# Down projection of 128 expert chunks with the tokens on the partitions: stationary z, weights moving 512 wide, and a final norm by token

## The reference

```python
def peer_ffn(x, w_q, sub_keys, u_tab, v_tab):      # x is already normed
    ...
        gate = jax.nn.softmax(best_s, axis=-1)     # 8 heads x 16 experts a token
        ug = u_tab[eidx]
        vg = v_tab[eidx]
        hpre = jnp.einsum("nd,nhkd->nhk", xc, ug).astype(f32)
        act = (gate * jax.nn.gelu(hpre, approximate=False)).astype(x.dtype)
        return jnp.einsum("nhk,nhkd->nd", act, vg)

def second_block(x, ...):
    ...
        x = x + peer_ffn(h, ...)
    return rms_norm(x, norm_final)                 # x / sqrt(mean(x*x) + 1e-6) * norm_final
```

## Time and profile before

| | |
|---|---|
| median of 3 runs | 2049.94 us (2047.15 to 2049.99) |
| the profiled execution's own time | 2039.93 us |
| its span | 2037.9 us |
| mean granted TensorE clock | 0.943 of full speed |
| busy, share of the span | PE 93%, PEld 90%, DVE 70%, ACT 43%, POOL 1% |
| down chunks 0 to 63 (third stage) | from 1627.15 us |
| down chunks 64 to 127 (last stage) | 1831.98 to 2023.76 us |
| behind the last down matmul | 14.1 us |

### The profile page before, as it was taken

One profiled execution on the slowest core, in us unless ns is written; L12 is line 12 of the kernel. 1 busy time (PEld: TensorE's weight loads), 2 busy tenths in 40 slices (PEclk: granted clock), 3 DMA queues, 4 the chain that ended last, 5 costly groups with the idle time before them and its releaser, 6 DMA issues.

```text
span 2037.9 us, 41749 instructions
## 1 busy us (share of the span) xinstructions
PE 1889.6 (93%) x15336; PEld 1833.0 (90%) x15336; DVE 1424.0 (70%) x2437; ACT 874.7 (43%) x1317; POOL 19.3 (1%) x38
## 2 busy tenths in 40 slices
PE   7979997999799969997789979999999999999997
PEld 7969996988799959986679979999999999999997
DVE  5668886844688863447766549996888889994554
ACT  4333443443343335365444444455444344444443
POOL 0000000010000000000100000000000000000000
PEclk9989997976899989987999989999999999999999
DMA  5525553420455524430026624455444445554553
GB/s 199 185 98 183 181 181 100 156 93 12 164 185 185 182 87 144 135 114 1 1 83 202 200 95 145 165 165 185 166 165 166 164 150 168 167 165 167 176 176 109
DMA packets 80276, 293.70 MB, mean 144 GB/s; under 512 B 8960, under 2 KB 9120, under 8 KB 79824
## 3 DMA queue, kind: packets, MB, share of 16 engines
q1 hardware_dynamic: 79632, 289.96, 43.2%
q0 software_dynamic: 576, 2.79, 0.4%
HBM read 291.67 MB, written 1.05 MB: 144 GB/s over the span
## 4 chain that ended last, share of the span: by engine, by line
PE 81%; DVE 14%; ACT 3%; issue 2%; DMA 0%; DVEq 0%; ACTq 0%
PE ps L421 23%; PE ps L422 22%; PE ps L423 22%; DVE m L395 3%; PE ps L427 3%; PE ps L462 2%; PE ps L1492 1%; DVE m L1394 1%; DVE m L514 1%; PE ps L752 1%; DVE m L1390 1%; ACT m L383 1%; PE ps L751 1%; DVE m L1398 1%; DVE m L508 1%
## 5 line engine op out<-in xcount | busy, mean ns | idle before, releaser
L421 PE MATMUL ps<-m,m 128*128 128x256 f32 x4336 | 1252.7, 289 | 69.2 <-DVE m L522 33.8
L422 PE MATMUL ps<-m,m 128*128 128x256 f32 x4336 | 1235.0, 285 | 0.0
L423 PE MATMUL ps<-m,m 128*128 128x256 f32 x4336 | 1234.4, 285 | 0.0
L395 DVE TENSOR_TENSOR m<-m,m 128x1024 fp32r<-128x1024 f32 x546 | 663.1, 1222 | 432.1 <-ACT m L383 430.5
L421 PEld LDWEIGHTS ps<-m,m 128*128 128x128 f32 x4336 | 840.5, 194 | 83.6 <-issue 53.1
L422 PEld LDWEIGHTS ps<-m,m 128*128 128x128 f32 x4336 | 840.8, 194 | 0.6 <-issue 0.2
L423 PEld LDWEIGHTS ps<-m,m 128*128 128x128 f32 x4336 | 840.0, 194 | 0.0
L383 ACT ACTIVATE m<-m 128x1024 fp32r<-128x1024 f32 x546 | 576.1, 1056 | 472.5 <-PE ps L423 471.1
L1531 ACT ACTIVATE m<-ps 128x256 f32 (+1 forms) x128 | 49.2, 384 | 198.6 <-PE ps L423 198.5
L427 PEld LDWEIGHTS ps<-m,m 128*128 128x128 f32 (+1 forms) x412 | 64.3, 232 | 31.2 <-issue 11.4
L427 PE MATMUL ps<-m,m 128*128 128x128 f32 (+1 forms) x412 | 74.8, 338 | 14.1 <-ACT m L877 10.8
(11 more groups left out here) (198 smaller groups left out, 1131.2 us busy)
## 6 DMA issues: line engine op xcount, KB each, us to landing
m<-stream SPq DMA_DIRECT2D x546, 512.0 KB, 3.3
m<-alibi_t POOLq DMA_DIRECT2D x1, 1536.0 KB, 9.6
m<-con SPq DMA_DIRECT2D x1, 1353.0 KB, 10.1
m<-xT SPq DMA_DIRECT2D x1, 1024.0 KB, 4.9
y<-m SPq DMA_DIRECT2D x4, 256.0 KB, 2.4
m<-wcmpk POOLq DMA_DIRECT2D x1, 512.0 KB, 4.1
m<-wcmpv POOLq DMA_DIRECT2D x1, 512.0 KB, 4.8
m<-par SPq DMA_DIRECT2D x1, 178.0 KB, 5.4
```

Of the source, the lines that this page charges most:

```text
L395: nc.vector.tensor_tensor(w_lo[:, r, :], raw[:, r, :], w_hi[:, r, :].bitcast(F32), ALU.subtract)\
L421: nc.tensor.matmul(out, lhs[0], rhs[0], start=start, stop=False, **kw)
L422: nc.tensor.matmul(out, lhs[0], rhs[1], start=False, stop=False, **kw)
L423: return nc.tensor.matmul(out, lhs[1], rhs[0], start=False, stop=stop, **kw)
```

## The change

1. **Down turned round.** `down_tokens` replaces `down` for the 128 expert chunks. A 128-token half of z is stationary and the weights stream, 512 features wide: for each half c of the tokens, z hi with w hi, z hi with w lo, z lo with w hi, each over two halves of the features. That is 12 matmuls a chunk in place of 24, over the same number of columns. The four banks then hold tokens on the partitions.
2. **x by token.** `x_tokens_pe` puts x into these banks first, with 16 plain fp32 matmuls against the identity, behind the wait for the first z and ahead of the first chunk. `residual_dve` at the end goes.
3. **z ahead of the weights.** On ACT, z of chunk n is copied first and the hi part of weight chunk n + 1 is split behind it; before, the split stood ahead. DVE's splits in the last stage are one chunk earlier to match (`DOWN0 - 2` for `DOWN0 - 1`).
4. **Take in short runs.** The view of `emap` has the 8 tokens inside (runs of 8 floats), and PSUM is read in steps of 64 floats instead.
5. **Sum and norm by token.** ACT squares each half of the tokens and sums along the free dimension in the same instruction, the half c = 0 as soon as the last chunk has finished it; DVE's scale and inverse and ACT's root are then one column each, and four DVE instructions read PSUM and write y. The final norm's weights come as a row for every partition (`fin_row`, 512 KB), loaded by POOL's queue once the down chunks begin.

```diff
+    def x_tokens_pe(pe):
+        for c in range(2):
+            for k in range(KD):
+                nc.tensor.matmul(acc[:, 2 * c + k // 4, k % 4 * P:k % 4 * P + P], x[:, k, c * P:c * P + P], ident,
+                                 start=k % 4 == 0, stop=False, skip_group_check=True)
+
+    def down_tokens(pe, slot, src, final):
+        for c in range(2):
+            z = [v[:, c * P:c * P + P] for v in src]
+            for lhs, rhs, last in ((z[0], w_hi, False), (z[0], w_lo, False), (z[1], w_hi, final)):
+                for h in range(2):
+                    ins = nc.tensor.matmul(acc[:, 2 * c + h, :], lhs, rhs[:, slot, h * 512:h * 512 + 512],
+                                           start=False, stop=last, skip_group_check=True)
+            if final:
+                ins.then_inc(tok_done, 1)
+        if not final:
+            ins.then_inc(chunk_done, 1)
+
+    def final_act(act):
+        for c in range(2):
+            act.wait_ge(tok_done, c + 1)
+            nc.scalar.activation(y_out[:, c, :], acc_tok[:, c, :], ACT.Square, accum_out=y_sum[:, c:c + 1])\
+                .then_inc(tok_sum, 1)
+        for c in range(2):
+            act.wait_ge(tok_mean, c + 1)
+            nc.scalar.activation(y_r[:, c:c + 1], y_mean[:, c:c + 1], ACT.Sqrt).then_inc(tok_rms, 1)
+
+    def final_dve(dve):
+        for c in range(2):
+            dve.wait_ge(tok_sum, c + 1)
+            nc.vector.tensor_scalar(y_sum[:, c:c + 1], y_sum[:, c:c + 1], 1.0 / D, EPS, ALU.mult, ALU.add)\
+                .then_inc(tok_scaled, 1)
+            dve.wait_ge(tok_scaled, c + 1)
+            nc.vector.reciprocal(y_mean[:, c:c + 1], y_sum[:, c:c + 1]).then_inc(tok_mean, 1)
+        dve.wait_ge(s_fin, 16)
+        for c in range(2):
+            dve.wait_ge(tok_rms, c + 1)
+            for h in range(2):
+                f = slice(h * 512, h * 512 + 512)
+                nc.vector.scalar_tensor_tensor(y_out[:, c, f], acc_tok[:, c, f], y_r[:, c:c + 1], fin_row[:, f],
+                                               ALU.mult, ALU.mult).then_inc(y_normed, 1)
...
-        v = emap[:, half * HALF:half * HALF + HALF, bass.ds(st.lin(GT), GT)]
-        return v.rearrange("p a t -> p t a")
+        return emap[:, half * HALF:half * HALF + HALF, bass.ds(st.lin(GT), GT)]
...
-        nc.vector.scalar_tensor_tensor(v, ps[:, 6 + st.mod(2), :].rearrange("p (t a) -> p t a", t=GT), 1.0 / GSCALE, v, ALU.mult, ALU.mult)\
+        nc.vector.scalar_tensor_tensor(v, ps[:, 6 + st.mod(2), :].rearrange("p (t a) -> p a t", t=GT), 1.0 / GSCALE, v, ALU.mult, ALU.mult)\
...
-        down(pe, arrived(pe, st, a, b + DOWN0), ez[st.mod(2, a, b)], n == 0, n == NKEY - 1)
+        if n == 0:
+            x_tokens_pe(pe)
+        down_tokens(pe, arrived(pe, st, a, b + DOWN0), ez[st.mod(2, a, b)], n == NKEY - 1)
...
         def z(st, gates=None):
             if st.s >= 2:
-                walk_act(act, st, 1, DOWN0 - 2)
+                act.wait_ge(chunk_done, st.lin(1, DOWN0 - 1))
             if gates is not None:
                 act.wait_ge(gm_taken, gates)
             nc.scalar.activation(ez[st.mod(2)][0], emap[:, st.lin(1), :], ACT.Copy).then_inc(ez_hi, 1)
+            if st.s >= 2:
+                split_hi(act, st, 1, DOWN0 - 2 + RING)
...
             if not last:
                 z_rest(st, 2, 2)
-            walk_dve(dve, st, 2, DOWN0)
+                walk_dve(dve, st, 2, DOWN0)
...
         def fourth(st):
             z_rest(st, 1, 0)
-            walk_dve(dve, st, 1, DOWN0 - 1)
+            walk_dve(dve, st, 1, DOWN0 - 2)
...
+            pool.wait_ge(chunk_done, DOWN0)
+            pool.dma_start(fin_row, fin2).then_inc(s_fin, 16)
```

More of the change, by code:

```diff
@@ L135, with build @@
 GSCALE = 2.0 ** 14
-def build(nc, stream, xT, par, con, alibi_t, wg, wcmpk, wcmpv, peT, subk, y):
+def build(nc, stream, xT, par, con, alibi_t, wg, wcmpk, wcmpv, peT, subk, fin2, y):
     def sem(name):
@@ L185, in build @@
     x = l_.take(KD, T)
+    O_HH = l_.at
     h_hi, h_lo = l_.take(KD, T, dt=F32R), l_.take(KD, T, dt=F32R)
@@ L205, in build @@
     acc = ps[:, 0:4, :]
+    acc_tok = acc.rearrange("p (c h) f -> p c (h f)", c=2)
     f_ = Area(END - 8 * T)
@@ L286, in build @@
     ez = [(z_hi, z_lo), (at(O_NORM, T, dt=F32R), at(O_NORM + T, T, dt=F32R))]
+    y_out = at(O_HH, 2, D)
+    fin_row = at(O_HH + 2 * D, D)
+    y_sum, y_mean, y_r = (at(O_HH + 3 * D + 8 * i, 2) for i in range(3))
     s_x = sem("x_loaded")
@@ L345, in build @@
     s_y = sem("y_stored")
+    tok_done, tok_sum, tok_scaled = sem("token_half_summed"), sem("token_square_sum"), sem("token_mean_square")
+    tok_mean, tok_rms, y_normed = sem("token_mean_recip"), sem("token_rms_recip"), sem("y_part_normed")
+    s_fin = sem("final_weight_loaded")
     NCH = CH["end"]
@@ L517, in norm_dve @@
         if hb is None:
-            dve.wait_ge(x_normed, KD if n < 7 else 2 * KD)
+            dve.wait_ge(x_normed, KD)
             return
@@ L1556, in peer_act @@
             z(Step(n))
-        for n in (NKEY, NKEY + 1):
-            walk_act(act, Step(n), 1, DOWN0 - 2)
     def peer_dve(dve, dc):
@@ L1614, in peer_dve @@
             fourth(Step(n))
-        dve.wait_ge(chunk_done, NCH)
     HP = {0: 0, 1: 4, 2: 8, 3: 12, 5: 16, 6: 20}
@@ L1625, in _ @@
             stream_all(sp)
[L1626 to L1629, removed]
+            for c in range(2):
+                for h in range(2):
+                    sp.wait_ge(y_normed, 2 * c + h + 1)
+                    sp.dma_start(y[:, c, h * 512:h * 512 + 512], y_out[:, c, h * 512:h * 512 + 512]).then_inc(s_y, 16)
+            sp.wait_ge(s_y, 16 * 4)
         @block.gpsimd
@@ L1689, in _ @@
             peer_pe(pe)
-            norm_pe(pe, 28)
         @block.scalar
@@ L1721, in _ @@
             peer_act(act)
-            norm_act(act, 7, x_part, 20)
+            final_act(act)
         @block.vector
@@ L1763, in _ @@
             peer_dve(dve, dc)
-            residual_dve(dve, dc)
-            norm_dve(dve, dc, 7, "fin2")
+            final_dve(dve)
 def constants():
@@ L1895, in lay_out @@
         "subk": w["peer_sub_keys_2"][0].transpose(0, 2, 1),
+        "fin2": np.broadcast_to(w["norm_final_2"][None], (P, D)),
     }
@@ L1908 @@
         args.append(nc.dram_tensor(name, a.shape, F32, kind="ExternalInput").ap())
-    y = nc.dram_tensor("y", (P, KD, T), F32, kind="ExternalOutput").ap()
+    y = nc.dram_tensor("y", (P, 2, D), F32, kind="ExternalOutput").ap()
     build(nc, *args, y)
     r = run(nc, [arrays], core_ids=[0])
-    return r.results[0]["y"].transpose(2, 1, 0).reshape(1, T, D)
+    return r.results[0]["y"].transpose(1, 0, 2).reshape(1, T, D)
```

## The result

The changed kernel takes 2026.22 us (median of 5; before 2049.15), a ratio of 0.9883 with a 95% interval of 0.9864 to 0.9902: some 24 us faster, 20 to 28 by the interval. The direction was right; 2026.2 lies above the range that was given (2001 to 2025), and the gain is about 60% of the 39.4 us that were forecast.

The account below looks back on a forecast made before the run. TensorE was taken to bound the kernel. Third stage -13.7, take -1.3, last stage -22.0, x +3.5 and end -5.9 summed to -39.4 us: 2010.5 us as a median, with a range of 2001 to 2025.

Parts of the forecast that it names:

- I take the 256-wide plain row, 0.219: Both down stages: a 512-wide fp32r matmul costs 0.219 us, as two 256-wide plain fp32 ones do for 512 streamed columns.
- It goes with the columns, 0.237: Rival, down's matmuls: excess over streaming time grows with columns, 0.237 us each, total -11.8 us; chance 6%.
- the fixed excess at 0.225: Rival, down's matmuls: the excess is a fixed time per matmul, 0.225 us each, total -30.2 us; chance 16%.
- the lower bound: DVE's take of the gate map: 0.7 us expected, from 0.68 in runs to about 1.04; saves 1.3 us at stage starts.
- The wait for z: Last stage: z stood behind the weights' split, costing 0.13 us a chunk; with z first, no wait is left.
- the +3.5 of x: Start of down: x's 16 plain fp32 matmuls stand behind the wait for z, nothing hides them, +3.5 us.
- the parts that the working lists up to the roots: The end: drain 0.2, Square 1.01, sum's read 0.19, table load 1.28, two roots of 0.2 each; given as 2.9 us.
- The ring: Rival, weight stream: chunks arriving at 180 GB/s (2.91 us) would leave nothing of the turn, 2035 us; chance 3%.
- 1.5 us for the clock: Last stage's start: the first chunk runs at 1.2 GHz behind its wait, counted as 1.5 us before and after.
- The turn alone gives 24 x 0.1185 - 2.63 = 0.21 a chunk of it, the order 0.13: Last stage: its -22.0 us divided per chunk between turning down round and putting z ahead of the weights.
- Neighbours' writes: Rival, down: ACT and DVE writing neighbouring slots slow the weight stream; at 0.260 us a matmul, 2074 us; chance 3%.
- stay at 1.35 us: Rival, third stage: PSUM's step costs what SBUF's saved, DVE sets about 6.05 us a step, 2018 us; chance 4%.

Follow-up runs that it names:

- x ahead of the wait: The changed kernel with x's 16 matmuls issued before the wait for the first z; median 2022.43 us against 2026.86 for the changed kernel beside it.
- the order: The kernel before with only z's copy moved ahead of the weights' split, down not turned; ratio 0.9968.
- Alone, the turn: The changed kernel with the old order of z and weights and the old take, x and end by token kept; ratio 0.9948 against the kernel before.
- the 384-wide kernel: The changed kernel streaming only 384 of each 512 weight columns in down, a quarter of its output left out; 0.1756 us from start to start.
- The 128-wide kernel: The changed kernel streaming only 128 of each 512 weight columns in down, the rest of its output left out; 0.2134 us start to start at low clock.
- the 256-wide kernel: The changed kernel with down's weights moving 256 wide, 24 matmuls a chunk, nothing left out; 0.1198 us start to start, 406.55 us to the end.

## Why the prediction was wrong

All differences are from the two traces, from the last batch of the second stage on; the stretches of the forecast are put together from its terms.

| | forecast | measured |
|---|---|---|
| third stage, 31 steps | -13.2 | -4.3 |
| start of down: x, take, the first step | +2.4 | +3.1 |
| last stage with its start | -22.7 | -14.3 |
| end | -5.9 | -5.5 |
| sum | -39.4 | -21.0 |

**The step that failed** is the size of one term, "I take the 256-wide plain row, 0.219, since it streams the same columns beside one load". It measured 0.2320. In the last stage this is 768 x 0.013 = 10.0 us, and in the third 31 x (6.127 - 5.84) = 8.9: 18.9 us, about the whole miss in the traces (18.4). The reason given with it, that the excess shows only where the streaming is about as short as the load, rested on the low clock's 0.213 with nothing over. That row can't tell the readings apart: at 1.2 GHz a column takes 0.83 ns, behind which a stream at 0.44 ns a column is hidden as well. The trace of x ahead of the wait has 512-wide fp32r matmuls at the low clock, and they are 0.427 us apart, again 512 columns at 1.2 GHz with nothing over. The plain rows were the nearest in columns and in loads, but not of the same kind, and the kind was what counted. Had the kind been weighed, the 256-wide fp32r row would have led: the rival "It goes with the columns, 0.237" was given 6% and a total of -11.8, the fixed excess at 0.225 16% and -30.2; the truth lay between them, 0.005 below the one and 0.007 above the other, and was none of the cases that were priced.

**What held.** Step by step: TensorE bounds both stages, also after the change. The take costs 0.68 us, the lower bound, and is hidden as said (-1.3 alone). The wait for z came from the split ahead of it; without it TensorE's row is unbroken, 183.8 us alone where the working has 183.5. x and the first two chunks together take 3.6 us more than these chunks did before, for the +3.5 of x alone. The end measured 8.64 for 8.2; the parts that the working lists up to the roots add up to 3.1 and not to its 2.9, and 2.9 is what they took, while DVE's four and the time behind them took 0.2 more each. `fin_row` cost nothing that a trace shows. The ring and DVE were not met.

**What partly held.** I counted 1.5 us for the clock at the last stage's start; in the changed kernel it stayed up, so that its last stage is 178.2 and not 179.7. That is luck and not insight, since behind the same idle time it fell with x ahead of the wait. "The turn alone gives 24 x 0.1185 - 2.63 = 0.21 a chunk of it, the order 0.13" treated the two as additive. Alone, the turn gave 0.04 a chunk in the last stage (2.4 us of 64 chunks) and the order 0.12, together 0.21, of which 0.02 is the clock.

**The other rivals.** Neighbours' writes don't slow the stream: the pace doesn't change when they pause. The take didn't stay at 1.35 us. The ring held ACT up at 218 GB/s, in the 384-wide kernel, and not at the 177 of the changed one.

## What to carry to other kernels

Price a wider matmul from a row of the same number format, and the excess over its streaming time at first in proportion to the columns; what is surely saved by widening is the fixed part, here some 0.008 us a matmul. When an engine is sped up that hardly waits, ask which chain of the others is nearly as long: here the turn was worth 2 us in the last stage until z was moved ahead of the weights' split. And work that is added for a new layout belongs into a stretch in which its engine is idle anyway: ahead of the wait, and not behind it, x was hidden and the clock stayed up there, for 3.75 us in all.

## What the runs showed of the hardware

- fp32r streams more slowly than plain fp32 and f16 on the same tiles: 0.44 ns a column against 0.42 (0.4292 us for 1024 columns, 0.2158 for 512), and some 0.008 us more a matmul.
- At 128 columns it isn't the stream that sets fp32r's pace. The 128-wide kernel ran its first chunks at the full clock (granted 1.00); 24 matmuls last 2.87 us, less one duration of 0.27 and over 23 distances 0.113 each. Streaming 128 columns at 2.4 GHz would take 0.053, and the line of the wider ones gives 0.064.

```profile
1640.39 2.87 PE L479 MATMUL ps<-m,m 128*128 128x128 f32 x24
```

This is the first of the two expectations on record, 0.107 to 0.12. At the low clock it is 0.2134, just as for 256 columns in the earlier trace rows. That it is the load of 128 fp32r columns, which would then last about as long as 256 streamed ones, is argued from this and not shown by itself.
- In the same kernel the granted clock fell to 0.50, the level of 1.2 GHz, at 1649.30 us and stayed there to the end of the run. Before that TensorE had waited for 0.27 and 0.89 us; behind it, it was busy for all but 0.24 of the next 180.70 us and without a break in the last stage.

```profile
1643.11:1649.30 6.19, 5.03 (x66) 4.69 (x65) 5.71 (x9) 4.50 (x7) 0.00 (x0) 1.00 0.31 91
1649.30:1830.00 180.70, 180.46 (x1195) 180.13 (x1194) 161.45 (x271) 79.50 (x116) 0.00 (x0) 0.50 0.53 177
```

In the 256-wide kernel the granted clock was 1.00 in both stages. Why it stayed low here isn't shown. The kernel as a whole took 2006 us with a quarter of the columns, so narrow matmuls gained little here, most of them at the low clock.
- DVE read PSUM in steps of 256 bytes no slower than in runs (0.684 us for 512 elements, against the 0.68 of line 1195), while steps in SBUF cost it much (1.354 at 1 KB, 0.978 for 480 at 64 bytes). The rule of the Trainium skill that I had set against this part ("SBUF — State Buffer", Door 1: The DMA port swizzle (why `[64,N]` ≈ `[32,N]`)) agrees on SBUF's side. Of PSUM it says that non-contiguous access slows matmuls; for VectorE's reads, to which I had carried it over, this run shows no such cost.
- Behind the same 1.95 to 1.96 us of idleness the granted clock was 0.53 for the next 3.2 us in one kernel (both traces of x ahead of the wait) and 1.00 in the other (both traces of the changed kernel). What decides isn't shown.
